# Moving the turned copies of indices and gates, and the attention's division, from VectorE to ScalarE

## The reference

```python
scores = einsum('bshd,bmhd->bhsm', q, k) * MEM_HEAD_DIM ** -0.5
p = softmax(scores, axis=-1)
o = einsum('bhsm,bmhd->bshd', p, v)
...
s_top, i_top = top_k(key_scores, 16)            # per head and half of the key
best, c_idx = top_k(s_top[0][:, None] + s_top[1][None, :], 16)
expert = i1 * 128 + i2                          # 8 heads x 16 picks a token
gates = softmax(best, axis=-1)
act = einsum('bthkd,btd->bthk', u[expert], x)
out = einsum('bthk,bthkd->btd', gates * gelu(act), v[expert])
```

## Time and profile before

| | |
|---|---|
| median of 3 runs | 4087.89 us (4086.88 to 4088.87) |
| span of the profiled execution | 4073.8 us |
| gather loop begins (first u gather) | 1338.40 us |
| first dense matmuls of the key halves' choice | about 2700 us |
| 32 copies of one gathered tile, DVE | 3.88 + 3.69 us |
| L1843 on DVE | 8 times 1239 ns |
| L1868 on DVE, both kinds | 224 copies, 24.4 + 23.3 us |

### The profile page before, as it was taken

How to read it: one execution, slowest core, us unless ns; L and a number is a source line. 1 busy time by engine, 2 the same in 40 slices (tenths; PEclk the granted TensorE clock), 3 DMA queues, 4 the chain that set the end, 5 groups by cost and what they waited for, 6 DMA issues and landing times.

```text
span 4073.8 us, 39536 instructions
## 1 busy us (share of the span) xinstructions
PE 3137.5 (77%) x13938; PEld 1964.3 (48%) x13938; DVE 2154.4 (53%) x4742; ACT 840.7 (21%) x2473; POOL 1898.9 (47%) x1592
## 2 busy tenths in 40 slices
PE   8999969998897173655546364569999999999994
PEld 5778856565474031312223031247555567555551
DVE  2340057676301868586776857686334348343334
ACT  1321023232111121222222122222111112111112
POOL 1242200000000667777776777664655554555555
PEclk8999979999998586777768586757999996999997
DMA  2322242121060799999999999976999995999998
GB/s 86 124 93 88 93 167 70 55 64 61 16 244 6 281 342 326 344 337 336 324 354 328 342 327 351 361 274 222 409 409 409 409 409 178 383 409 409 409 409 306
DMA packets 313628, 1075.98 MB, mean 264 GB/s; under 512 B 33248, under 2 KB 56672, under 8 KB 311792
## 3 DMA queue, kind: packets, MB, share of 16 engines
q0 software_dynamic: 221184, 805.40, 53.0%
q1 hardware_dynamic: 92272, 268.37, 17.4%
HBM read 1037.47 MB, written 36.18 MB: 264 GB/s over the span
## 4 chain that ended last, share of the span: by engine, by line
PE 28%; DMA 15%; POOL 13%; DVE 7%; issue 5%; ACT 1%; POOLq 0%; ACTq 0%; DVEq 0%
DMA u_ring<-in_u_dram,idx 9%; DMA v_ring<-in_v_dram,idx_v 7%; POOL v_ring L1422 6%; PE acc L1454 6%; POOL u_ring L1410 6%; PE small L1564 5%; PE wide L1576 4%; PE small L1552 3%; PE small L1508 3%; PE wide L1493 3%; PE wide L1479 2%; DVE u_ring L1776 1%; PE small L1461 1%; PE wide L1518 1%; DVE work L2037 1%
## 5 line engine op out<-in xcount | busy, mean ns | idle before, releaser
L1410 POOL DMA_INDIRECT u_ring<-in_u_dram,idx x768 | 841.4, 1096 | 1250.1 <-DVE idx L2000 788.9
L1776 DVE CUSTOM_DVE_ANT_0 u_ring<-u_ring,h 128x1024 f32<-128x1024 f32 x768 | 933.2, 1223 | 773.3 <-DMA u_ring<-in_u_dram,idx 768.7
L1422 POOL DMA_INDIRECT v_ring<-in_v_dram,idx_v x768 | 907.5, 1182 | 507.8 <-PE acc L1454 300.1
L1454 PE MATMUL acc<-v_ring,spread_w 128*32 128x512 f32 x3072 | 523.2, 814 | 641.9 <-DMA v_ring<-in_v_dram,idx_v 618.2
L1454 PEld LDWEIGHTS acc<-v_ring,spread_w 128*32 128x32 f32 x3072 | 105.3, 133 | 988.1 <-issue 932.5
L1564 PE MATMUL small<-pwq 128*128 128x256 f32 x2048 | 471.9, 384 | 1.6 <-ACT memory_tables L1701 1.6
L1576 PE MATMUL wide<-pwq,memory_tables 128*128 128x512 f32 x1024 | 463.4, 596 | 0.0
L1564 PEld LDWEIGHTS small<-pwq 128*128 128x128 f32 x2048 | 389.7, 192 | 123.9 <-issue 76.0
L1576 PEld LDWEIGHTS wide<-pwq,memory_tables 128*128 128x128 f32 x1024 | 191.7, 190 | 218.3 <-issue 213.6
L1644 ACT ACTIVATE spread_w<-comb,w_v 128x32 f32<-128x32 f32 x768 | 194.4, 311 | 248.4 <-PE acc L1454 174.9
L694 PE MATMUL mix_bank<-w_out,mixT 128*128 128x512 f32 x512 | 226.2, 598 | 2.4 <-ACT mixT L884 2.4
(11 more groups left out here) (291 smaller groups left out, 4052.4 us busy)
## 6 DMA issues: line engine op xcount, KB each, us to landing
pwq<-in_uT_dram SPq DMA_DIRECT2D x128, 512.0 KB, 9.0
pwq<-in_v_dram SPq DMA_DIRECT2D x128, 512.0 KB, 6.8
w_nat<-in_w_nat_dram SPq DMA_DIRECT2D x6, 2048.0 KB, 7.9
nat_dram<-stage SPq DMA_DIRECT2D x48, 256.0 KB, 2.2
u_ring<-in_u_dram,idx POOLq DMA_INDIRECT x768, 6.7
v_ring<-in_v_dram,idx_v POOLq DMA_INDIRECT x768, 6.7
scanT_dram<-stage SPq DMA_DIRECT2D x22, 512.0 KB, 2.9
w_tr<-in_w_tr_dram SPq DMA_DIRECT2D x18, 512.0 KB, 4.0
```

The lines of the kernel that those rows point to most:

```text
L1410: pool.indirect_dma_start(out=u_ring[:, g % U_RING, :], out_offset=None, in_=peer_u, in_offset=bass.IndirectOffsetOnAxis(ap=idx[:, t % KEP ...
L1422: pool.indirect_dma_start(out=v_ring[:, g % V_RING, :], out_offset=None, in_=peer_v, in_offset=bass.IndirectOffsetOnAxis(ap=idx_v[:, t % K ...
L1454: last = pe.matmul(acc[c * QUAD:(c + 1) * QUAD, half * 512:(half + 1) * 512], spread_w[:, slot, :], v_ring[:, slot, half * 512:(half + 1) ...
L1776: dve.tensor_tensor_reduce(out=row, in0=row, in1=h2[:, s, :], scale=1.0, scalar=0.0, op0=ALU.mult, op1=ALU.add, accum_out=act_u[:, (n // T ...
```

## The change

The 32 turned copies go from DVE to ACT, as Copy activations, and with them the writing of `idx`: DVE now writes the expert numbers as floats into `experts_f`, a part of `vals`, and ACT makes the integers of `idx` from it, and `idx_v` as 16 copies. ACT does so behind the spread of the slot in which DVE does chunk 38 or 39. The semaphores `experts_ready` and `gates_made` go from DVE to ACT; `idx_ready`, `idx_v_ready` and `gates_ready` are now given by ACT. ACT's stage 2 waits for `experts_ready` in place of `idx_ready`. DVE gets two waits, for ACT to have read the former tile's `vals` and `gexp`. In the front DVE takes only the reciprocal of the sums (stage 16), and ACT scales the four heads' 128x256 blocks (stage 17). The counts of `front_step` shrink by what DVE no longer does.

```diff
-FRONT_STEPS = 28
-FIRST_STEPS = 22
+FRONT_STEPS = 26
+FIRST_STEPS = 21
+PLACES_CHUNK = 38
...
+        experts_f = vals[:, 0:PHEADS, :].rearrange("p h k -> p (h k)")
...
@@ ACT
                     if n == 2:
                         if f > 0:
-                            act.wait_ge(idx_ready, f + 1)
+                            act.wait_ge(experts_ready, f + 1)
...
+                    if n == 17:
+                        act.wait_ge(pinv_ready, f + 1)
+                        for h in range(HEADS_CA):
+                            at = probs[:, h * MEM:(h + 1) * MEM]
+                            last = act.activation(at, at, ACT.Copy, scale=pinv[:, h:h + 1])
+                        last.then_inc(probs_ready, 1)
...
+                def regroup(to, source):
+
+                    for r in range(SIDE):
+                        for c in range(SIDE):
+                            last = act.activation(
+                                to[r * QUAD:(r + 1) * QUAD, :].rearrange("p (b c) -> p b c", c=SIDE)[:, :, c],
+                                source[c * QUAD:(c + 1) * QUAD, :].rearrange("p (b r) -> p b r", r=SIDE)[:, :, r],
+                                ACT.Copy)
+                    return last
+
+                def keep_places(f, hs, turn):
+
+                    picks, at = slice(hs[0] * TOPK, (hs[-1] + 1) * TOPK), f % KEPT
+                    act.wait_ge(experts_ready, turn)
+                    act.activation(idx[:, at, picks], experts_f[:, picks], ACT.Copy).then_inc(idx_ready, 1)
+                    regroup(idx_v[:, at, picks], experts_f[:, picks]).then_inc(idx_v_ready, 1)
+
+                def keep_gates(f, hs, turn):
+
+                    picks = slice(hs[0] * TOPK, (hs[-1] + 1) * TOPK)
+                    act.wait_ge(gates_made, turn)
+                    regroup(gates_v[:, f % KEPT, picks], gexp[:, :, :].rearrange("p h k -> p (h k)")[:, picks]
+                            ).then_inc(gates_ready, 1)
...
+                        if t == 0 and n == PLACES_CHUNK + 1:
+                            keep_places(0, range(FIRST_HEADS, PHEADS), 2)
+                        if t == 0 and n == GATES_CHUNK + 1:
+                            keep_gates(0, range(FIRST_HEADS, PHEADS), 2)
...
+                        if PLACES_CHUNK in chunks and f < GATHERED:
+                            keep_places(f, range(PHEADS), f + 2)
+                        if GATES_CHUNK in chunks and f < GATHERED:
+                            keep_gates(f, range(PHEADS), f + 2)
...
@@ DVE
                     if n == 16:
                         dve.wait_ge(probs_exp, f + 1)
-                        link(dve.reciprocal(pinv[:, :], psums[:, :]), 2)
-                        p4 = probs.rearrange("p (h m) -> p h m", m=MEM)
-                        dve.tensor_tensor(p4, p4, pinv[:, :].unsqueeze(2).to_broadcast([P, HEADS_CA, MEM]),
-                                          ALU.mult).then_inc(probs_ready, 1)
+                        dve.reciprocal(pinv[:, :], psums[:, :]).then_inc(pinv_ready, 1)
...
                         if c == 0:
                             dve.wait_ge(keyscores_ready, f + 1)
                             dve.wait_ge(h2_ready, f + 1)
+                            if turn > 1:
+                                dve.wait_ge(idx_v_ready, min(turn - 1, GATHERED + 1))
...
+                        if turn > 1:
+                            dve.wait_ge(gates_ready, min(turn - 1, GATHERED + 1))
                         dve.tensor_tensor(gexp[:, h0:h1, :], best[:, h0:h1, :],
...
-                    if c == 38 and f < GATHERED:
-                        dve.scalar_tensor_tensor(idx[:, kept_at, picks], ihalf[0][:, picks], float(NKEYS),
-                                                 ihalf[1][:, picks], ALU.mult, ALU.add).then_inc(idx_ready, 1)
-                        dve.wait_ge(idx_ready, turn)
-                        regroup(idx_v[:, kept_at, picks], idx[:, kept_at, picks]).then_inc(idx_v_ready, 1)
+                    if c == PLACES_CHUNK:
+                        if f < GATHERED:
+                            dve.scalar_tensor_tensor(experts_f[:, picks], ihalf[0][:, picks], float(NKEYS),
+                                                     ihalf[1][:, picks], ALU.mult, ALU.add).then_inc(experts_ready, 1)
...
-                        if f < GATHERED:
-                            regroup(gates_v[:, kept_at, picks], gexp[:, :, :].rearrange("p h k -> p (h k)")[:, picks]
-                                    ).then_inc(gates_ready, 1)
```

More of the change, by code:

```diff
@@ L1258, in attend_and_retrieve @@
         probs_ready = sem("probs_ready")
+        pinv_ready = sem("pinv_ready")
         probsT_made, probsT_ready = sem("probsT_made"), sem("probsT_ready")
@@ L1726, in _ @@
                 gate_exps(range(FIRST_HEADS), 1)
+                keep_places(0, range(FIRST_HEADS), 1)
+                keep_gates(0, range(FIRST_HEADS), 1)
                 def norm3(t):
@@ L1847, in front @@
                         link(dve.scalar_tensor_tensor(pre2, h1[:, :], ALPHA, wide[:, D:2 * D], ALU.mult,
-                                                      ALU.add), 3)
-                        norm_stats(pre2, 0, front_step, at + 4).then_inc(var2_ready, 1)
+                                                      ALU.add), 2)
+                        norm_stats(pre2, 0, front_step, at + 3).then_inc(var2_ready, 1)
                     if n == 34:
@@ L1856, in front @@
                     if n == 35:
-                        dve.wait_ge(front_step, at + 6)
+                        dve.wait_ge(front_step, at + 5)
                         dve.tensor_tensor(pre2, pre2, ln[:, 0, :], ALU.mult).then_inc(front_step, 1)
                     if n == 36:
-                        dve.wait_ge(front_step, at + 7)
+                        dve.wait_ge(front_step, at + 6)
                         dve.tensor_tensor(h2[:, 0, :] if f == 0 else pre2, pre2, ln[:, 1, :],
                                           ALU.add).then_inc(h2_ready, 1)
[L1864 to L1871, removed]
                 def top_picks(f, s, at, c, hs, turn):
-                    link = link_from(at)
+                    link = link_from(at - 1)
                     G, h0, h1 = len(hs), hs[0], hs[-1] + 1
@@ L1998, in top_picks @@
                             link(dve.tensor_reduce(ihalf[half][:, picks], w3, AX, ALU.add), 22 + 3 * half + pos)
[L1999 to L2005 removed]
+                    if c == PLACES_CHUNK:
+                        if f < GATHERED:
+                            dve.scalar_tensor_tensor(experts_f[:, picks], ihalf[0][:, picks], float(NKEYS),
+                                                     ihalf[1][:, picks], ALU.mult, ALU.add).then_inc(experts_ready, 1)
+                        else:
+                            dve.sem_inc(experts_ready, 1)
                     if c == GATES_CHUNK:
@@ L2011, in top_picks @@
                             idx[:, kept_at, :].bitcast(F32).rearrange("p (h k) -> p h k", k=TOPK))
-                        link(dve.tensor_tensor(gates[:, h0:h1, :], gexp[:, h0:h1, :],
-                                               ginv[:, h0:h1].unsqueeze(2).to_broadcast([P, G, TOPK]),
-                                               ALU.mult), 28 + pos)
-                        if f < GATHERED:
-                            regroup(gates_v[:, kept_at, picks], gexp[:, :, :].rearrange("p h k -> p (h k)")[:, picks]
-                                    ).then_inc(gates_ready, 1)
-                        else:
-                            dve.sem_inc(picks_ready, 1)
+                        dve.tensor_tensor(gates[:, h0:h1, :], gexp[:, h0:h1, :],
+                                          ginv[:, h0:h1].unsqueeze(2).to_broadcast([P, G, TOPK]),
+                                          ALU.mult).then_inc(gates_made if f < GATHERED else picks_ready, 1)
                 def hots(b, q):
```

5 lines of the change are left out of this document (2 added, 3 removed).

## The result

The changed kernel takes 4127.31 us as the median of 4 runs (4122.57 to 4133.36), where the kernel before took 4088.38 (4086.88 to 4092.44) beside it: a ratio of 1.0096, 95% interval 1.0076 to 1.0115. It is slower. Run again on another chip it took 4134.77 against 4085.27, a ratio of 1.0116 (1.0093 to 1.0140).

What follows compares the result with a forecast made beforehand. No engine is full; at tile boundaries the front's chain over PE, ACT and DVE bounds the kernel. 42.2 - 4.2 + 4.0 + 0.4 = 42.4 us on the 4073.8 span, plus 14.1 around it: 4130 us, range 4106 to 4148.

Steps and rivals of the forecast that it cites:

- 1, DVE's freed time is worth nothing at the boundaries: At the five tile boundaries DVE loses 7.57 us of copies each, worth nothing since it already waits 4.10 us for PE.
- 2, the copies: ACT's turned copies: a set of 16 takes 3.50 us, as 32 elements cost no more than 4.
- rival D: At the boundaries ACT's copies go at a spread's full 0.31 us, 14.6 us more in all, 4145 us; chance 0.12.
- Rival E: ACT overlaps the copies, 1.9 us for a set of 16, not 3.50; 16 us less in all, 4114; chance 0.08.
- 3, the delay: Five boundaries: copies ahead of slot 95's spread put the combine 7.92 us after the expert numbers, 42.2 us in all.
- 4, given back: Fronts 3 and 4: PE's waits for v rows ahead of the second attention product go, -4.2 us.
- 5, the division: In eight fronts ACT's four scalings end about 0.5 us later than DVE's multiply did, +4 us.
- 6, the first indices: POOL's first gather waits 0.3 us for one copy more, no loss at slot 39; +0.4 us for both.
- The base: Whole-kernel sum: made on the profiled span of 4073.8 us, with 14.1 us around it added unchanged.
- The signs named in advance: At boundaries: combine released by ACT, DVE's wait for scores from 4.10 to about 15 us, numbers to scores near 13.

## Why the prediction was right

The forecast was 4130 us and 1.0% slower; it was 4127.31 and 0.96%, and 1.16% on the second chip. The mechanism was the forecast one, but some terms were off and made up for each other. By points:

**1, DVE's freed time is worth nothing at the boundaries.** Right in substance: off DVE and out of the way the copies bring 0.1 to 0.3%. At the start it was worth more than I took: the first dot starts 4.43 us after its gather's issue and not 6.84, and lies 2.0 us earlier from front 0's copy on. Front 1's copy is at the same distance from front 0's as before, within 0.2 us, so that this was lost again on the way to slot 39; the DMA share between 1340 and 1440 us is 0.93.

**2, the copies.** The term that was mis-sized. I took 3.50 us for a set, by the argument that 32 elements cost no more than 4; they take 4.30. The rows of 32x4 and of 128x32 had both stood at 0.21 to 0.22 us apart, but neither had 32 elements with a step of four. At 0.269 us apart the copies are past the 0.25 that I had named as the sign of rival D; but they don't reach D's 0.31, and cost 8 us over the five boundaries where D had 14.6. So D was right in direction and about half right in size. Rival E (under 0.15 apart) falls. The Trainium skill, page "ScalarE: Activation LUTs", section "What ACT_TABLE_LOAD costs", has a fixed part, 0.833 ns an element and an overlap, from which I estimated 0.12 us apart. The trace shows 0.269, and 0.237 with neighbouring columns: the pace is not the rule's, though the 0.8 ns an element of neighbouring columns (226 less 210 ns over 20 elements) agrees with its 0.833.

**3, the delay.** 9.48 to 9.52 us at all five boundaries where 7.92 were forecast, 50.0 us in sum and not 42.2. The 7.8 us between are five times 1.56, nearly all of it the two sets of point 2, 0.8 us longer each. That the delay passes to the end: right, by the sets made twice.

**4, given back.** 5.6 us in fronts 3 and 4 (8.80 to 4.78, 6.23 to 4.60) where 4.2 were forecast, and 1.5 more at front 4's scores. The picks between the fronts took 4.8 us more; I had nothing for that, and its cause is not shown.

**5, the division.** Right: 5.46 us from the maximum to the transposes in each front, where four of five had 4.98 to 5.16 before; 0.3 to 0.5, against 0.5. Front 3 had 5.60, so nothing was lost there, and over the eight fronts it is 2.9 us in place of 4.0.

**6, the first indices.** The first gather starts 0.77 us after the numbers do (1338.34 to 1339.11) where it was 0.50, 0.3 later as forecast; front 1 begins with no loss.

**The base.** I added the 14.1 us between the profiled span and the median as time around the span. That was wrong: the changed kernel's profiled execution took 4128.33 us with a span of 4126.5, so that 1.8 us lie around it. With the same 1.8, the profiled execution of the kernel before was some 12 us faster than the median. The sum still started from the right total, since span and rest add up to the median. By spans the forecast was 42.4 us and the two traces are 52.7 apart; by medians it is 39 and, on the second chip, 49.5. The closeness of 4130 to 4127 is thus part luck: the term of point 3 was 8 us short, the picks' 4.8 us weren't in the sum, and the first measurement came out lower than the second, of 4134.77.

**The signs named in advance.** The combine is released by ACT at all five boundaries, as forecast. The wait for the scores grew to 16.15 and 16.04 us in fronts 3 and 5, near the 15 forecast, but to only 8.84 in fronts 2, 4 and 6: there DVE idles earlier, 9.1 to 12.7 us of waiting for the gelu, which the prediction had not followed. At the first boundary it is 15.9 us from the numbers to the scores and not 13. Copies over 0.25 us apart are the one sign of being wrong that came true.

## What to carry to other kernels

Before work moves to an engine with idle time, look at what stands behind its new place in that engine's order and who waits for that: here 9 us of small copies on an engine busy 21% held back one 0.3 us operation until 9.5 us after the numbers, and with it the other engines' chain by 7.3 to 12.0 us each time. An engine that runs ahead of the others is a buffer; a wait put into its list takes all of the lead, not just the wait's own work, as the 16 gate copies showed that cost as much as 33. Put such work behind the last thing that the chain wants of the engine and under the longest stretch that it spends elsewhere, in pieces where other short work is due; then compare with the version in which it isn't moved, for the freed time itself may be worth next to nothing, here 0.1 and 0.3% by the two ratios.

## What was not expected of the hardware

- A Copy of 32 partitions by 32 elements with a step of four takes 258 ns on ScalarE and 226 with neighbouring elements; with 12 elements 222 and 210. In sets of 16 they start 0.269 and 0.237 us apart, so they don't overlap, while spreads of 128x32 with a pointer scale go at about 0.22 with a length of 0.31.
- Four Copies of 128x256 with a pointer scale take 1.70 us, with a mean of 505 ns each, so they do overlap.
- The same kernel on another chip took 4143.44 us and not 4085 to 4089, with single runs from 4126.78 to 4160.69.
